# Routed experts: the order of the 128-slot and the 64-slot turns

## Chip, cores and metric

One core of one Trainium2 chip runs the kernel. The metric is the device time in microseconds. The kernel before took 2576.52, 2579.29 and 2581.18 us in three runs; the median is 2579.29 us.

## The reference, cut to what matters

The network is two blocks. The first has two layers of a hybrid mixer, a memory cross-attention and a feed-forward part; the second is an mLSTM/LRU block with product-key retrieval. The feed-forward part of the second layer is a mixture of 8 experts over 256 tokens of width 1024. Each token goes to its two best experts:

```
logits = (xt @ w_router).astype(jnp.float32)
top_vals, top_idx = lax.top_k(logits, TOP_K)          # TOP_K = 2 of N_EXPERTS = 8
...                                                   # softmax over the two gives the shares
y_e = (silu(x_e @ w_gate[e]) * (x_e @ w_up[e])) @ w_down[e]    # D_EXPERT = 3584
h = h + sum over the token's two experts of share * y_e
```

The last line and the one before it are the meaning of `moe_swiglu` in short form. The order in which the experts are computed does not enter into the result, apart from rounding of the sum.

## The kernel before, in words

**Turns.** The eight experts are computed in eight turns, 0 to 7. Each turn streams one expert's weights as 42 tiles of 1 MiB (`EXP_TILES`): 28 for gate and up (`GATE_UP`, four to a chunk of 512 hidden features, 7 chunks) and 14 for down (`DOWN`). Tile 0.0 is the first tile of turn 0.

**Two programs.** In a large turn (128 slots) the tokens are split in a high and a low part, each 128 columns wide, and every product of a weight tile is three matmuls: high by high (L862), high by low (L863), low by high (L864), 12 matmuls of 512 columns per tile. In a small turn (64 slots) the high and the low part of 64 tokens share one stationary operand of 128 columns (`xe_high` holds both, `he_pairs` the hidden ones), so that two matmuls are enough (L968, L969), 8 per tile; `folded_transposes` (L982) then adds the two halves. Both programs stream the same 42 tiles.

**A tile's way.** The SyncE queue issues the load of a tile (L1465) into one of 7 buffers (`RING`), as soon as TensorE has used the tile that was there seven tiles earlier. ScalarE rounds it to the high part (L1857), VectorE makes the low part (L2573), TensorE multiplies. ScalarE and VectorE are written out tile by tile with a lead of four tiles (`EXP_AHEAD`): at step j they first treat tile j+4 and then do the turn's other work of that step.

**Other work of a turn.** VectorE prepares the list of the next turn's tokens (`slot_lists`), GpSimd fetches their rows from `x_tokens` (L1570), TensorE transposes them, and VectorE copies them as high and low parts (`transposed_tokens`, L2593 and L2595), at step 33 of a large turn and step 31 of a small one. The width of these copies is set by the turn that comes next: 64 tokens or 128. At the end of a turn ScalarE scales the outputs (L1931 in a large turn, L1899 in a small one) and GpSimd adds them to `y_tokens` (L1578), in one scatter after a large turn and two after a small one.

**Order.** `ranks` (L2488 on) ranks the experts by their number of tokens. Expert 0 always has rank 0. `holds` marks which expert a turn holds; `order` gives SyncE the expert of each turn. The four experts of rank 0 to 3 get 128 slots and are turns 0 to 3; the other four get 64 slots and are turns 4 to 7. On each engine the large turns are one hardware loop (on VectorE a loop of three and one turn apart) and the small ones another (on VectorE and ScalarE with the last one apart). Tokens that find no slot would send the kernel into a second pass, which did not run here.

Of the kernel before, what the change touches and what calls it, by code (L numbers as in the profile page):

```python
# [13 lines left out]
P = 128  # L14
# [6 lines left out]
FF, N_EXP, EXP_W = 2816, 8, 3584  # L21
# [55 lines left out]
CHUNKS = EXP_W // 512  # L77
# [12 lines left out]
LIST_CHUNK = 3  # L90
CLEARS = 3
LARGE, HALF = 4, P // 2
EXP_MARKS = 2 * CHUNKS + DOWN - 1


# [131 lines left out]
def two_blocks(nc, t, out):  # L227
    with ExitStack() as ctx:
# [162 lines left out]
        room, order = small[:, 112:120], small[:, 120:128].bitcast(I32)  # L391
        turn_place_all = small[:, 202:202 + TB * (N_EXP + 1)].rearrange("p (b e) -> p b e", b=TB)
        turn_place, turn_share = turn_place_all[:, :, 0:N_EXP], pairs_of(32)
        rank_key, rank, excess, order_f = (std_row[:, 8 * i:8 * i + 8] for i in range(4))
        def by_rank(a):
            return a.rearrange("p (r e) -> p r e", r=N_EXP)
        holds, above, numbers = by_rank(std_row[:, 64:128]), by_rank(mean_row[:, 0:64]), by_rank(mean_row[:, 64:128])
# [164 lines left out]

        def rows_added(e, small=True):

            if small:
                return 16 * (CLEARS + LARGE + 2 * (e - LARGE))
            return 16 * (CLEARS + e)

        block = ctx.enter_context(nc.Block())

# [2 lines left out]
        def _(pe):  # L573
# [341 lines left out]
            def experts(n):  # L915
# [138 lines left out]
                pe.wait_ge(g.took_sems["v"], g.took["first", 4])  # L1054
                g.open_turns()
                if n == 0:
                    with pe.Fori(0, LARGE) as e:
                        turn(e, False)
                    pe.wait_ge(routing_ready, 1)
                    overflow = pe.value_load(extra_flag[0:1, 0:1], min_val=0, max_val=1)  # L1060
                    with pe.Fori(LARGE, N_EXP) as e:
                        turn(e, True)
                else:
                    with pe.Fori(0, N_EXP) as e:
                        turn(e, False)
# [463 lines left out]
        def _(pool):  # L1529
# [35 lines left out]
            pool.wait_ge(x_stored, 16)  # L1565
            g = passes[0]
            for e in range(N_EXP):
                kind, m = "s_" if e >= LARGE else "", HALF if e + 1 >= LARGE else P
                pool.wait_ge(g.took_sems["v"], g.took[kind + "lists"] + e * g.takes["v"])
                pool.indirect_dma_start(out=x_rows[0:m, :], out_offset=None, in_=x_tokens,  # L1570
                                        in_offset=bass.IndirectOffsetOnAxis(ap=token_at[0:m, :], axis=0)).then_inc(rows_gathered, 16)
                if e == N_EXP - 1:
                    break
                pool.wait_ge(g.took_sems["a"], g.took[kind + "down", 1] + e * g.takes["a"])
                for half in ((slice(0, HALF), slice(HALF, P)) if kind else (slice(0, P),)):
                    if half.start:
                        pool.wait_ge(y_done, rows_added(e) + 16)
                    pool.indirect_dma_start(out=y_tokens, out_offset=bass.IndirectOffsetOnAxis(ap=put_at[0:half.stop - (half.start or 0), :], axis=0), in_=ye[half, :],  # L1578
                                            in_offset=None, compute_op=ALU.add).then_inc(y_done, 16)
# [25 lines left out]
        def _(act):  # L1605
# [238 lines left out]
            def experts(n):  # L1844
# [90 lines left out]
                if n:  # L1935
# [4 lines left out]
                        expert(e, True)  # L1940
                    expert(N_EXP - 1, False)
                    return None
                with act.Fori(0, LARGE) as e:
                    expert(e, True)
                act.wait_ge(routing_ready, 1)
                overflow = act.value_load(extra_flag[0:1, 0:1], min_val=0, max_val=1)
                with act.Fori(LARGE, N_EXP - 1) as e:
                    small_expert(e, True)
                small_expert(N_EXP - 1, False)
                return overflow  # L1950

# [216 lines left out]
        def _(dve):  # L2168
# [310 lines left out]
            def eight(a, axis):  # L2479
                return a.unsqueeze(axis).to_broadcast([P, N_EXP, N_EXP])  # L2480
# [8 lines left out]
            def ranks():  # L2489

                iota8 = iota[:, 0:N_EXP]
                dve.wait_ge(dve_took, G.took["places"])
                step.now(dve.scalar_tensor_tensor(rank_key, counts, float(N_EXP), iota8, ALU.mult, ALU.subtract))
                step.now(dve.memset(rank_key[:, 0:1], 1.0e6))
                step.now(dve.tensor_tensor(above, eight(rank_key, 1), eight(rank_key, 2), ALU.is_gt))
                step.now(dve.tensor_reduce(rank, above, AX.X, ALU.add))
                step.then(dve.tensor_tensor(holds, eight(rank, 1), eight(iota8, 2), ALU.is_equal))
                step.now(dve.tensor_scalar(room, rank, float(LARGE) - 0.5, float(P - HALF), ALU.is_lt, ALU.mult))
                step.then(dve.tensor_scalar(room, room, float(HALF), None, ALU.add))
                step.now(dve.tensor_tensor(numbers, holds, eight(iota8, 1), ALU.mult))  # L2500
                step.then(dve.tensor_reduce(order_f, numbers, AX.X, ALU.add))
                step.now(dve.tensor_tensor(excess, counts, room, ALU.subtract))
                step.then(dve.tensor_copy(order, order_f))
                step.now(dve.tensor_reduce(most, excess, AX.X, ALU.max))
                dve.tensor_scalar(extra_flag[:, 0:1], most, 0.0, None, ALU.is_gt).then_inc(routing_ready, 1)
                dve.memset(turn_place_all[:, :, N_EXP:], -1.0)
                step.now(in_turns(turn_place, place))
# [14 lines left out]
            def experts(n):  # L2522
# [63 lines left out]
                def transposed_tokens(e, done, key, next_small):  # L2586

                    m = HALF if next_small else P
                    for i in range(KT // 2):
                        done((key, i))  # L2590
                        bank, s = pair(bank_in((key, i)), 2, P)[:, :, 0:m], slice(2 * i, 2 * i + 2)
                        high, low = xe_high[:, s, 0:m], xe_high[:, s, HALF:P] if next_small else xe_low[:, s, :]
                        dve.tensor_copy(high, bank).then_inc(g.x_high, 1)  # L2593
                        dve.wait_ge(g.x_high, 5 + e * (KT // 2) + i + 1)
                        took_it(dve.tensor_tensor(low, bank, high.bitcast(F32), ALU.subtract))  # L2595
# [9 lines left out]
                    dve.wait_ge(g.filled_ready, e + 1)  # L2605
                    took_it(dve.tensor_tensor(put_at, found[:, 2:3], rest_row, ALU.add))  # L2606

                def small_expert(e, follow):
                    def done(key):
                        dve.wait_ge(g.group_done, g.after[key] + e * g.in_turn)  # L2610

                    def multiply(c):
                        dve.wait_ge(g.activated, (e - LARGE) * CHUNKS + c + 1)
                        up = bank_in(("s_hidden", c))[:, 4 * HALF:8 * HALF].rearrange("p (a b) -> p a b", a=4)
                        took_it(dve.tensor_tensor(he_half[:, 4 * c:4 * c + 4, :], up, activated, ALU.mult))

                    def hidden(c):

                        dve.wait_ge(g.hidden_rounded, (e - LARGE) * CHUNKS + c + 1)
                        s = slice(4 * c, 4 * c + 4)  # L2620
                        dve.tensor_tensor(he_pairs[:, s, HALF:P], he_half[:, s, :], he_pairs[:, s, 0:HALF].bitcast(F32),
                                          ALU.subtract).then_inc(g.hidden_split, 1)

                    for j in range(EXP_TILES):
                        if j + EXP_AHEAD < EXP_TILES:
                            low_part(e, j + EXP_AHEAD)
                        elif follow:
                            low_part(e + 1, j + EXP_AHEAD - EXP_TILES)
                        c, step_ = divmod(j, 4)
                        if 0 < c < CHUNKS and step_ == 2:  # L2630
                            multiply(c - 1)
                        elif 1 < c <= CHUNKS and step_ == 0:
                            hidden(c - 2)
                        elif j == 1:
                            expert_columns(e, True)
                        elif j == 3:
                            expert_places(e)
                        elif j == 4 * LIST_CHUNK + 3:
                            slot_lists(e, done, "s_lists", True)
                        if j == GATE_UP:  # L2640
                            multiply(CHUNKS - 1)
                        elif j == GATE_UP + 2:
                            hidden(CHUNKS - 1)
                        elif j == GATE_UP + 3:
                            transposed_tokens(e, done, "s_gather", True)

                def expert(e, follow, next_small=False):
                    def done(key):
# [53 lines left out]
                dve.tensor_tensor(fold, ident[:, 0:HALF], ident[:, HALF:P], ALU.add)  # L2702
                dve.wait_ge(list_consts_ready, 1)
                dve.wait_ge(share_ready, 1)
                with dve.Fori(0, LARGE - 1) as e:
                    expert(e, True)
                dve.wait_ge(routing_ready, 1)
                overflow = dve.value_load(extra_flag[0:1, 0:1], min_val=0, max_val=1)
                expert(LARGE - 1, True, True)
                with dve.Fori(LARGE, N_EXP - 1) as e:  # L2710
                    small_expert(e, True)
                small_expert(N_EXP - 1, False)
                return overflow

            for l in range(DEPTH):
# [494 lines left out]
```

## Time and profile before

| | |
|---|---|
| median of three runs | 2579.29 us |
| span of the profiled execution | 2569.7 us |
| the three runs' own times | 2576.52, 2579.29, 2581.18 us; the page does not say which was profiled, so 6.8 to 11.5 us lie around its span |
| TensorE busy over the span | 2384.0 us (93%) |
| VectorE busy | 2009.7 us (78%) |
| ScalarE busy | 1256.6 us (49%) |
| moved by DMA | 786.10 MB, mean 306 GB/s |

The page's second part cuts the span in 40 slices of 64.2 us. The turns of the experts lie in slices 11 to 25, from about 656 to 1565 us. The span runs from the first to the last instruction; the device time also has what lies before and behind these. "Busy" of TensorE counts a matmul from its start to its modelled end, so a share of 100% says that it never stood idle, not that it computed at its peak.

### The profile page before, as it was taken

The page shows a single profiled execution, that of the slowest core. Times are in us where ns is not written, and L with a number is a line of the kernel's source. Part 1 is how long each engine was busy: PE and PEld are TensorE (multiplying, and loading weights), DVE is VectorE, ACT ScalarE, POOL GpSimd, SP SyncE. Part 2 cuts the span into 40 slices and gives each one's busy share as a digit, 9 for nine tenths or more (in the row PEclk, how much of TensorE's full clock was granted, in tenths as well). Part 3 has the DMA queues.
Part 4 walks back from the last instruction along what each step waited for, and adds up shares of the span by engine and source line. Part 5 has one row for each costly group of instructions (what it writes and reads, how often), then busy time and mean ns, then how long its engine had stood idle before and what let it go on. Part 6 is the DMA issues. An engine that isn't in the chain of part 4 may idle for free.

```text
span 2569.7 us, 32436 instructions
## 1 busy us (share of the span) xinstructions
PE 2384.0 (93%) x12064; PEld 1861.5 (72%) x12064; DVE 2009.7 (78%) x3035; ACT 1256.6 (49%) x1302; POOL 285.7 (11%) x305
## 2 busy tenths in 40 slices
PE   9999999999999999999899899999999987878786
PEld 8899999899788888877677678888985443323332
DVE  5766754865898888989999999666668887887875
ACT  2554332363777777878888886216421111111111
POOL 0000000000000000000000000000013433333341
PEclk9999999999999999999999999999999998899999
DMA  8454654541899999999999997531769999999997
GB/s 246 155 189 133 196 193 140 164 159 67 334 375 380 377 375 370 390 374 415 414 415 408 414 416 265 153 92 47 244 248 421 421 421 421 421 422 421 422 421 294
DMA packets 238447, 786.10 MB, mean 306 GB/s; under 512 B 24369, under 2 KB 154545, under 8 KB 162289
## 3 DMA queue, kind: packets, MB, share of 16 engines
q1 hardware_dynamic: 198000, 504.46, 53.1%
q0 software_dynamic: 39184, 276.58, 26.3%
q10 hardware_dynamic: 1136, 3.43, 0.3%
q8 instruction: 73, 1.20, 0.2%
q14 instruction: 54, 0.43, 0.0%
HBM read 777.08 MB, written 7.34 MB: 305 GB/s over the span
## 4 chain that ended last, share of the span: by engine, by line
PE 58%; DMA 22%; DVE 10%; issue 5%; ACT 4%; POOL 0%; DVEq 0%; ACTq 0%; SPq 0%
DMA dense_weights<-in_peer_rows,work 14%; DMA weight_tiles<-in_moe_tiles 7%; PE banks L862 7%; PE banks L864 7%; PE banks L863 7%; PE banks L728 5%; PE banks L1327 5%; PE banks L682 5%; PE banks L683 4%; PE banks L686 4%; PE banks L660 4%; DVE weight_tiles_low L2573 3%; ACT weight_tiles_high L1857 2%; PE banks L592 1%; PE banks L968 1%
## 5 line engine op out<-in xcount | busy, mean ns | idle before, releaser
L2573 DVE TENSOR_TENSOR weight_tiles_low<-weight_tiles,weight_tiles_high 128x2048 fp32r<-128x2048 f32 x335 | 761.5, 2288 | 72.7 <-ACT weight_tiles_high L1857 67.1
L1857 ACT ACTIVATE weight_tiles_high<-weight_tiles 128x2048 fp32r<-128x2048 f32 x332 | 635.5, 1918 | 149.4 <-DMA weight_tiles<-in_moe_tiles 144.7
L1327 PE MATMUL banks<-dense_weights,work 128*128 128x512 f32 x888 | 415.4, 618 | 57.9 <-DVE work L3104 57.5
L1327 PEld LDWEIGHTS banks<-dense_weights,work 128*128 128x128 f32 x888 | 173.0, 199 | 289.9 <-issue 201.1
L3094 DVE CUSTOM_DVE_ANT_0 dense_weights<-dense_weights,banks 128x1024 f32<-128x1024 f32 x222 | 266.5, 1217 | 68.2 <-DMA dense_weights<-in_peer_rows,work 67.3
L2205 DVE TENSOR_TENSOR weight_tiles_low<-weight_tiles,weight_tiles_high 128x2048 fp32r<-128x2048 f32 x93 | 212.2, 2289 | 129.2 <-ACT weight_tiles_high L1623 129.0
L2119 ACT ACTIVATE work<-work,small 128x2 f32<-128x2 f32 x129 | 38.1, 295 | 540.4 <-DVE work L3094 540.2
L1599 POOL DMA_INDIRECT dense_weights<-in_peer_rows,work x222 | 208.6, 940 | 588.0 <-DVE work L3050 315.0
L968 PE MATMUL banks<-weight_tiles_high,gathered_parts 128*128 128x512 f32 x448 | 183.8, 410 | 27.3 <-DVE weight_tiles_low L2573 26.8
L1623 ACT ACTIVATE weight_tiles_high<-weight_tiles 128x2048 fp32r<-128x2048 f32 x93 | 177.4, 1910 | 56.2 <-PE banks L864 29.5
L682 PE MATMUL banks<-weight_tiles_high 128*128 128x256 f32 x800 | 189.4, 281 | 5.1 <-issue 3.1
L683 PE MATMUL banks<-weight_tiles_high,weight_tiles_low 128*128 128x256 f32 x800 | 187.8, 280 | 0.0
L862 PE MATMUL banks<-weight_tiles_high,gathered_parts 128*128 128x512 f32 x448 | 176.4, 394 | 1.6 <-DVE gathered_parts L2584 1.1
L969 PE MATMUL banks<-weight_tiles_low,gathered_parts 128*128 128x512 f32 x448 | 175.6, 392 | 0.0
L864 PE MATMUL banks<-weight_tiles_high,gathered_parts 128*128 128x512 f32 x448 | 174.7, 390 | 0.0
L863 PE MATMUL banks<-weight_tiles_low,gathered_parts 128*128 128x512 f32 x448 | 174.4, 389 | 0.0
L682 PEld LDWEIGHTS banks<-weight_tiles_high 128*128 128x128 f32 x800 | 152.7, 191 | 5.7 <-issue 3.3
L683 PEld LDWEIGHTS banks<-weight_tiles_high,weight_tiles_low 128*128 128x128 f32 x800 | 152.6, 191 | 0.2
L968 PEld LDWEIGHTS banks<-weight_tiles_high,gathered_parts 128*128 128x128 f32 x448 | 84.0, 188 | 68.9 <-DVE weight_tiles_low L2573 52.8
L3104 DVE TENSOR_SCALAR work<-ident,work 128x128 f32<-128x128 f32 x256 | 79.2, 355 | 46.6 <-ACT work L2119 45.0
L1570 POOL DMA_INDIRECT work<-x_tokens,lists x8 | 18.0, 2248 | 848.0 <-DVE lists L2606 848.0
L728 PE MATMUL banks<-normed,weight_tiles 128*128 128x256 f32 (+1 forms) x512 | 111.7, 380 | 0.0
(508 smaller groups left out, 4467.9 us busy)
## 6 DMA issues: line engine op xcount, KB each, us to landing
weight_tiles<-in_moe_tiles SPq DMA_DIRECT2D x336, 1024.0 KB, 8.3
weight_tiles<-in_w_in SPq DMA_DIRECT2D x38, 1024.0 KB, 5.5
weight_tiles<-in_w_xkv SPq DMA_DIRECT2D x16, 1024.0 KB, 5.7
weight_tiles<-in_ffn_w_gate SPq DMA_DIRECT2D x11, 1024.0 KB, 5.3
weight_tiles<-in_ffn_w_up SPq DMA_DIRECT2D x11, 1024.0 KB, 5.3
weight_tiles<-in_ffn_w_down SPq DMA_DIRECT2D x11, 1024.0 KB, 5.0
weight_tiles<-in_w_xq SPq DMA_DIRECT2D x8, 1024.0 KB, 5.2
weight_tiles<-in_w_xo SPq DMA_DIRECT2D x8, 1024.0 KB, 5.2
```

What stands on the lines that cost most here:

```text
L682: pe.matmul(o, high[:, k, n_], high_x(k), start=(k == 0 and i == 0), stop=False)
L683: pe.matmul(o, low[:, k, n_], high_x(k), start=False, stop=False)
L728: mm = pe.matmul(bank[0:m, i * SEQ:(i + 1) * SEQ], w[:, k, i * P:i * P + m], x(k), start=(k == 0), stop=(k == KT - 1))
L862: pe.matmul(o, a_high, b_high, start=start, stop=False)
L863: pe.matmul(o, a_high, b_low, start=False, stop=False)
L864: return pe.matmul(o, a_low, b_high, start=False, stop=stop)
L968: pe.matmul(o, pairs, high, start=start, stop=False)
L1327: mm = pe.matmul(halves[half], diag[(first + j) % 8], pair_row(first + j)[:, 1, half * 512:(half + 1) * 512], start=False, stop=end and j ...
L1857: act.activation(high_tile(j), raw_tile(j), ACT.Copy).then_inc(g.high, 1)
L2205: dve.tensor_tensor(low_tiles[:, n % RING, 0:size], raw_tiles[:, n % RING, 0:size], high_tiles[:, j % HIGH_RING, 0:size].bitcast(F32), ALU ...
L2573: dve.tensor_tensor(low_tile(j), raw_tile(j), high_tile(j).bitcast(F32), ALU.subtract).then_inc(g.split, 1)
L3094: ins = dve.tensor_tensor_reduce(u_row, u_row, tokens(b), 1.0, 0.0, ALU.mult, ALU.add, dots[:, c:c + 1])
```

## The change

The turns alternate: even turns run the large program, odd turns the small one. Every engine's two loops become one loop over pairs of turns (`PAIRS` = 4), on VectorE and ScalarE over three pairs with the last pair apart. Ranks 0 to 3 keep 128 slots and become turns 0, 2, 4, 6; ranks 4 to 7 keep 64 and become turns 1, 3, 5, 7. `ranks` gets two small operations more that work out the turn of a rank. `rows_added` counts scatters in the new order. The number of turns of each kind, of tiles, matmuls, gathers and scatters is the same.

```diff
@@ rows_added
-            if small:
-                return 16 * (CLEARS + LARGE + 2 * (e - LARGE))
-            return 16 * (CLEARS + e)
+            return 16 * CLEARS + 24 * e - (8 if small else 0)
@@ TensorE
-                    with pe.Fori(0, LARGE) as e:
-                        turn(e, False)
+                    with pe.Fori(0, PAIRS) as p:
+                        turn(2 * p, False)
+                        turn(2 * p + 1, True)
                     pe.wait_ge(routing_ready, 1)
                     overflow = pe.value_load(extra_flag[0:1, 0:1], min_val=0, max_val=1)
-                    with pe.Fori(LARGE, N_EXP) as e:
-                        turn(e, True)
@@ GpSimd
-                kind, m = "s_" if e >= LARGE else "", HALF if e + 1 >= LARGE else P
+                kind, m = ("s_", HALF if e == N_EXP - 1 else P) if e % 2 else ("", HALF)
@@ ScalarE
-                with act.Fori(0, LARGE) as e:
-                    expert(e, True)
+                with act.Fori(0, PAIRS - 1) as p:
+                    expert(2 * p, True)
+                    small_expert(2 * p + 1, True)
                 act.wait_ge(routing_ready, 1)
                 overflow = act.value_load(extra_flag[0:1, 0:1], min_val=0, max_val=1)
-                with act.Fori(LARGE, N_EXP - 1) as e:
-                    small_expert(e, True)
+                expert(N_EXP - 2, True)
                 small_expert(N_EXP - 1, False)
@@ VectorE, ranks
-                step.then(dve.tensor_tensor(holds, eight(rank, 1), eight(iota8, 2), ALU.is_equal))
                 step.now(dve.tensor_scalar(room, rank, float(LARGE) - 0.5, float(P - HALF), ALU.is_lt, ALU.mult))
                 step.then(dve.tensor_scalar(room, room, float(HALF), None, ALU.add))
+                step.now(dve.tensor_scalar(late, rank, float(LARGE) - 0.5, float(N_EXP - 1), ALU.is_gt, ALU.mult))
+                step.now(dve.scalar_tensor_tensor(turn_at, rank, 2.0, late, ALU.mult, ALU.subtract))
+                step.now(dve.tensor_tensor(holds, eight(turn_at, 1), eight(iota8, 2), ALU.is_equal))
@@ VectorE, small_expert
-                            transposed_tokens(e, done, "s_gather", True)
+                            transposed_tokens(e, done, "s_gather", not follow)
@@ VectorE, experts
-                with dve.Fori(0, LARGE - 1) as e:
-                    expert(e, True)
+                with dve.Fori(0, PAIRS - 1) as p:
+                    expert(2 * p, True, True)
+                    small_expert(2 * p + 1, p, True)
                 dve.wait_ge(routing_ready, 1)
                 overflow = dve.value_load(extra_flag[0:1, 0:1], min_val=0, max_val=1)
-                expert(LARGE - 1, True, True)
-                with dve.Fori(LARGE, N_EXP - 1) as e:
-                    small_expert(e, True)
-                small_expert(N_EXP - 1, False)
+                expert(N_EXP - 2, True, True)
+                small_expert(N_EXP - 1, PAIRS - 1, False)
```

On TensorE, this is the end of the loop of large turns (turn 3's last matmul and what follows it) in the kernel before. L1060 reads the flag for the second pass; the matmuls behind it are turn 4's first ones.

```order
L863 MATMUL banks<-weight_tiles_low,work_parts 128x512
L864 MATMUL banks<-weight_tiles_high,work_parts 128x512
L937 REGISTER_ALU
L1057 REGISTER_ALU
L1057 COMPARE_AND_BRANCH
L1060 TENSOR_LOAD extra_flag
L1060 ISA x2
L1061 UNCONDITIONAL_BRANCH
L1061 ISA
L957 ISA
L968 MATMUL banks<-weight_tiles_high,gathered_parts 128x512
L969 MATMUL banks<-weight_tiles_low,gathered_parts 128x512
```

And in the changed kernel, at the same place of the program (the end of a large turn; its line numbers are lower by one):

```order
L862 MATMUL banks<-weight_tiles_low,work_parts 128x512
L863 MATMUL banks<-weight_tiles_high,work_parts 128x512
L936 REGISTER_ALU
L115 ISA
L956 ISA
L967 MATMUL banks<-weight_tiles_high,gathered_parts 128x512
L968 MATMUL banks<-weight_tiles_low,gathered_parts 128x512
```

The small turn's matmuls now follow each large turn inside the loop, and the branch back stands behind each small turn. The reading of the flag has moved behind the last turn.

On VectorE, this is step 31 of a small turn in its loop in the kernel before: the copies of the next turn's tokens between the low parts of two weight tiles (`gathered_parts` holds the tokens, `2x64` is two features' groups of 64 tokens).

```order
L2573 TENSOR_TENSOR weight_tiles_low<-weight_tiles,weight_tiles_high 128x2048
L2610 REGISTER_ALU
L2593 CAST gathered_parts<-banks 128x2x64
L2594 ISA
L2595 TENSOR_TENSOR gathered_parts<-banks,gathered_parts 128x2x64
L2610 REGISTER_ALU
L2593 CAST gathered_parts<-banks 128x2x64
L2594 REGISTER_ALU
L2595 TENSOR_TENSOR gathered_parts<-banks,gathered_parts 128x2x64
```

The same place in the changed kernel:

```order
L2573 TENSOR_TENSOR weight_tiles_low<-weight_tiles,weight_tiles_high 128x2048
L2610 REGISTER_ALU
L2593 CAST gathered_parts<-banks 128x256
L2594 ISA
L2595 TENSOR_TENSOR gathered_parts<-banks,gathered_parts 128x256
L2610 REGISTER_ALU
L2593 CAST gathered_parts<-banks 128x256
L2594 REGISTER_ALU
L2595 TENSOR_TENSOR gathered_parts<-banks,gathered_parts 128x256
```

The copies of a small turn in the loop are now 256 wide, since a large turn follows it; those of every large turn are 2x64 wide, which before was so for turn 3 alone.

## Rows read from the trace of the kernel before

**Rows 1.** The page, part 2: the span in 40 slices.
```profile
GB/s 246 155 189 133 196 193 140 164 159 67 334 375 380 377 375 370 390 374 415 414 415 408 414 416 265 153 92 47 244 248 421 421 421 421 421 422 421 422 421 294
```
**Rows 2.** Busy time of the engines in turns 1 to 7, one row per turn.
```profile
core 0: us, PE busy (x) PEld busy (x) DVE busy (x) ACT busy (x) POOL busy (x), PEclk, DMA share, GB/s
775.50:894.90 119.40, 119.40 (x550) 99.08 (x549) 107.24 (x74) 93.96 (x68) 3.01 (x2) 1.00 0.96 377
894.90:1014.30 119.40, 119.40 (x550) 99.08 (x549) 105.65 (x73) 92.49 (x67) 2.57 (x2) 1.00 0.98 375
1014.30:1133.70 119.40, 119.40 (x550) 99.08 (x549) 107.00 (x75) 94.51 (x69) 5.08 (x2) 1.00 0.98 377
1133.70:1239.40 105.70, 97.35 (x466) 77.15 (x464) 97.04 (x73) 88.06 (x70) 4.52 (x2) 0.98 1.01 411
1239.40:1347.30 107.90, 97.79 (x464) 75.28 (x464) 101.86 (x74) 91.92 (x72) 6.41 (x3) 1.00 1.01 414
1347.30:1455.60 108.30, 98.05 (x465) 75.43 (x464) 102.15 (x75) 91.91 (x72) 6.36 (x3) 1.00 1.01 413
1455.60:1564.80 109.20, 98.36 (x465) 76.92 (x465) 100.28 (x75) 88.13 (x71) 6.32 (x3) 0.98 0.95 386
```
**Rows 3.** TensorE's first gate matmul: turns 4, 5, 7 (first and last start, us).
```profile
L968 PE MATMUL banks<-weight_tiles_high,gathered_parts x114: 387/391/504, 1133.7 to 1239.9; 128*128 128x512 f32 x114
...
L968 PE MATMUL banks<-weight_tiles_high,gathered_parts x113: 387/393/504, 1239.3 to 1347.6; 128*128 128x512 f32 x113
...
L968 PE MATMUL banks<-weight_tiles_high,gathered_parts x112: 387/393/504, 1455.9 to 1528.3; 128*128 128x512 f32 x112
```
**Rows 4.** Tile loads (L1465), issue to landing: 1010 to 1133 us, then 1289 to 1397.
```profile
DMA to landing us min/median/max: 4.7/5.4/8.8
...
DMA to landing us min/median/max: 8.7/10.7/13.2
```
**Rows 5.** Timeline of TensorE from turn 3 into turn 4.
```profile
1133.44 0.39 PE L864 MATMUL banks<-weight_tiles_high,work_parts 128*128 128x512 f32 x1
1133.67 0.39 PE L968 MATMUL banks<-weight_tiles_high,gathered_parts 128*128 128x512 f32 x1
...
1148.86 0.50 PE L968 MATMUL banks<-weight_tiles_high,gathered_parts 128*128 128x512 f32 x1 [1.85 <-DVE weight_tiles_low L2573]
```
**Rows 6.** Stretches: turn 4's start and rest; two drops of the clock.
```profile
1133.70:1147.00 13.30, 13.12 (x57) 10.22 (x55) 9.16 (x9) 9.38 (x8) 1.76 (x1) 1.00 1.02 371
1147.00:1239.30 92.30, 84.16 (x409) 66.85 (x408) 87.79 (x65) 78.68 (x62) 2.76 (x1) 0.98 1.01 417
...
1226.80:1230.10 3.30, 3.30 (x10) 2.53 (x9) 3.30 (x2) 2.40 (x2) 0.00 (x0) 0.50 1.03 425
1551.10:1554.40 3.30, 3.17 (x8) 2.50 (x9) 3.30 (x3) 2.08 (x2) 0.00 (x0) 0.50 1.02 423
```
**Rows 7.** Timeline of VectorE: turn 0's token copies, then turn 5's.
```profile
753.82 0.42 DVE L2593 CAST gathered_parts<-banks 128x256 fp32r<-128x256 f32 x1
...
756.98 8.89 DVE L2573 TENSOR_TENSOR weight_tiles_low<-weight_tiles,weight_tiles_high 128x2048 fp32r<-128x2048 f32 x4
...
1329.93 0.28 DVE L2593 CAST gathered_parts<-banks 128x128 fp32r<-128x128 f32 x1
...
1332.03 20.02 DVE L2573 TENSOR_TENSOR weight_tiles_low<-weight_tiles,weight_tiles_high 128x2048 fp32r<-128x2048 f32 x9
```
**Rows 8.** Waits in turn 0 (656 to 775 us).
```profile
PE banks L862 <- DVE weight_tiles_low L2573: 0.5, 1, 0.5
```
**Rows 9.** Turn 0's start: `ranks` on VectorE, and TensorE's wait.
```profile
659.83 0.22 DVE L2497 TENSOR_TENSOR std<-std,iota 128x64 f32<-128x64 f32 x1
659.97 0.16 DVE L2498 TENSOR_SCALAR small<-std 128x8 f32<-128x8 f32 x1
...
664.41 8.90 DVE L2573 TENSOR_TENSOR weight_tiles_low<-weight_tiles,weight_tiles_high 128x2048 fp32r<-128x2048 f32 x4 [0.18 <-issue]
...
666.76 0.50 PE L862 MATMUL banks<-weight_tiles_high,gathered_parts 128*128 128x512 f32 x1 [0.55 <-DVE weight_tiles_low L2573]
```

More of the change, by code:

```diff
@@ L92 @@
 LARGE, HALF = 4, P // 2
+PAIRS = N_EXP // 2
 EXP_MARKS = 2 * CHUNKS + DOWN - 1
@@ L393, in two_blocks @@
         turn_place, turn_share = turn_place_all[:, :, 0:N_EXP], pairs_of(32)
-        rank_key, rank, excess, order_f = (std_row[:, 8 * i:8 * i + 8] for i in range(4))
+        rank_key, rank, excess, order_f, late, turn_at = (std_row[:, 8 * i:8 * i + 8] for i in range(6))
         def by_rank(a):
@@ L2606, in slot_lists, with small_expert @@
                     took_it(dve.tensor_tensor(put_at, found[:, 2:3], rest_row, ALU.add))
-                def small_expert(e, follow):
+                def small_expert(e, p, follow):
                     def done(key):
@@ L2612, in multiply @@
                     def multiply(c):
-                        dve.wait_ge(g.activated, (e - LARGE) * CHUNKS + c + 1)
+                        dve.wait_ge(g.activated, p * CHUNKS + c + 1)
                         up = bank_in(("s_hidden", c))[:, 4 * HALF:8 * HALF].rearrange("p (a b) -> p a b", a=4)
@@ L2617, in hidden @@
                     def hidden(c):
-                        dve.wait_ge(g.hidden_rounded, (e - LARGE) * CHUNKS + c + 1)
+                        dve.wait_ge(g.hidden_rounded, p * CHUNKS + c + 1)
                         s = slice(4 * c, 4 * c + 4)
```

## The prediction, made before the changed kernel ran

> **What bounds the kernel now.** I first read the page's slices for where the experts lie: in slices 12 to 18 the DMA rate stands near 377 GB/s and in slices 19 to 24 near 414 [rows 1]. Then I cut this stretch at the turns. A large turn takes 119.4 us and TensorE is busy for all of it; a small turn takes 105.7 to 109.2 us and TensorE is idle for 8.4 to 10.8 us of it [rows 2]. So the two programs have different limits. The large one is bound by TensorE: the DMAs bring 377 GB/s, and 411 to 414 GB/s in the small turns shows that they could bring more. The small one is bound by its supply: 42 tiles of 1.049 MB at 417 GB/s, the rate of the steady part of turn 4 [rows 6], are 105.6 us, and the scatters and gathers take the DMAs too. VectorE is close behind, busy for 102 of 108 us.
>
> Between the two lies the ring of 7 buffers. A buffer is loaded again when TensorE has used its tile, so a tile's round is 7 tiles long: 7 x 119.4 / 42 = 19.9 us in a large turn, 7 x 108.3 / 42 = 18.0 in a small one. Of this the load takes 5.4 us in a large turn and 10.7 in a small one, where loads queue [rows 4]. What is left, 14.5 against 7.3 us, is the time from landing to use, and the large turn's extra of 7.2 us is lead: tiles that are ready and wait for TensorE. A small turn behind a large one spends this lead. The trace has one such place, and it is the model for the change. TensorE goes from turn 3's last matmul to turn 4's first with no gap (1133.44, 1133.67: 0.23 us, the step of the stream), and its first wait of more than 0.2 us ends at 1148.86 [rows 5].
>
> **What the change is worth, part by part.**
>
> Small turn behind large. By first matmuls turn 4 takes 1239.3 - 1133.7 = 105.6 us, turn 5 takes 1347.6 - 1239.3 = 108.3, and turn 6 takes 1455.9 - 1347.6 = 108.3 [rows 3]. The lead is thus worth 2.7 us by the end of the turn. Its first seven tiles took 13.3 us in place of 18.0, which is 4.7 us saved, but in this stretch the DMAs moved only 371 GB/s, and 2.0 us are given back as the buffers run short [rows 6]. Before, turns 5, 6 and 7 stood behind a small turn. After, all four small turns stand behind a large one: 3 x 2.7 = 8.1 us saved.
>
> Large turn behind small. This is new in the trace three times (turns 2, 4, 6) and has two parts. One is the width of the token copies at the end of the small turn. Eight copies at 128x256 take 756.98 - 753.82 = 3.16 us, eight at 128x128 take 1332.03 - 1329.93 = 2.10 us [rows 7]. Behind these copies VectorE runs nine low parts back to back (20.02 us, 2.2 us each), which reach three tiles into the next turn [rows 7]; TensorE waits for each of them, so nothing hides the 1.06 us: the next turn's first tile is that much later. It costs 3 x 1.06 = 3.2 us. The large turns 0, 2 and 4 get narrower copies in exchange; there VectorE has the lead before it, and I count nothing for it (at most the same 3.2 us, at least nothing).
>
> The other part is the start of the large turn without a lead. A large tile takes TensorE 2.84 us (119.4 / 42). VectorE needs 107.2 / 42 = 2.55 us per tile with everything it does in a large turn, and the DMAs 1.049 / 417 = 2.5 us. Both are faster than TensorE, so from the first tile on it should find the next one ready and the lead should build by 0.3 us a tile, full before the turn ends (7.2 / 0.3 = 24 tiles of 42). Turn 0 shows such a start on VectorE's side: at 666.76 TensorE takes tile 0.4 right as its low part comes [rows 9], and up to the turn's end it waits for VectorE no more (one wait, 0.5 us) [rows 8]. What turn 0 does not show is a full DMA queue at the same time. I take nothing for this part. The lower bound is nothing, as there is no stall to remove in a large turn. The upper bound is that the whole lead has to be bought by waiting, 7.2 us a turn.
>
> ScalarE has at such a start 1.4 us of output scaling and perhaps the reload of an activation table; it has 25 us to spare in a large turn [rows 2] and is tiles ahead. I cost it at nothing, and if its cover went it would be inside the upper bound just named.
>
> `ranks`. Two small operations are added and one loses its overlap. Dependent ones of this size start some 0.14 us apart without a wait (659.83, 659.97) [rows 9] and somewhat more with one; three such steps are about 0.5 us. They stand before the low parts of tiles 0.4 to 0.7 (664.41), and TensorE waits 0.55 us there for tile 0.4 [rows 9]. So all of it goes on the path: 0.5 us, between 0.3 and 0.8. A TensorE-bound turn follows and cannot win it back.
>
> Moved at no cost: the flag's reading on TensorE now stands behind turn 7. TensorE's sequencer ran ahead of the matmuls at its old place, where no gap shows [rows 5]; at the new one I take nothing, at most 1 us. The number of scatters and gathers is the same, and so are their bytes; three of the large turns now start beside two scatters in place of one, with the same bytes.
>
> Sum: -8.1 + 3.2 + 0.5 = -4.4 us. The profiled execution's span of 2569.7 us would become 2565.3. What lies around the span is not touched, so the median of 2579.3 becomes 2574.9 us, 0.17% less.
>
> **The clock.** At VectorE's copies TensorE waits longest, and in turns 4 and 7 the granted clock then fell to 0.50, the 1.2 GHz level, for some 3.3 us; in turns 5 and 6 it did not [rows 2, 6]. It fell 13 us before the turn's end, where TensorE has time to spare, and turn 4 was still the shortest. The Trainium skill (TensorE: Matmul & The Clock Gate, "What's actually happening") has it that the clock is granted by recent activity. By that rule the wait that grows by 1.06 us makes drops likelier in three turns; where they fell before they cost nothing. A drop that reached into a large turn would cost half its length, 1.7 us.
>
> **The rivals.**
>
> *The lead is kept* (faster). If the 4.7 us of turn 4's first seven tiles are not given back, the three turns save 14.1 us and the sum is -14.1 + 3.7 = -10.4: 2568.9 us. For it: a small turn that starts early puts its loads into the queue early. Against it: turn 4 gave back 2.0 us, and the changed turns repeat it.
>
> *The large turn starves* (slower). TensorE, without a lead, waits at each place where VectorE does something else: the columns and picks at steps 4 and 6, the hidden parts, and the loads that two scatters hold up. It decides if tiles come slower than 2.84 us in the first ten tiles of turns 2, 4 and 6. With half of the bound, 3.6 us a turn, it is 10.8 us on the sum: +6.4, 2585.7 us; with all of it +17. For it: VectorE's margin is only 0.3 us a tile. Against it: the first turn [rows 8].
>
> *All is given back* (no change). The buffers' lead is one and the same time, and what the small turn spends the next large one has to load again, beside its own tiles. If the costs at the border are 1.5 us more per pair than my count, the whole is zero: 2579.3 us. The Trainium skill (DMA: Bandwidth & Descriptors, "Where 436 GB/s comes from") names a limit of some 358 GB/s on the HBM side for loads into SBUF. By that rule both programs would be bound by the same DMA rate and their order would be worth nothing, 2579.3 us. The trace disagrees: 414 GB/s in small turns, 377 in large ones with TensorE never idle [rows 2].
>
> That the change does not do what it says can be left out: turns, tiles and matmuls are the same, and no wait is tied to a turn's kind.
>
> **Chances and range.** Forecast 0.58, with its own range 2572 to 2578; no change 0.17; lead kept 0.12; starving 0.13. About 0.2%, 5.2 us, is what a measurement of this kernel can tell from no change; the three runs before spread over 4.7 us. The forecast's own range reaches over that bound on the faster side: 0.58 x 0.45 = 0.26, with the lead kept 0.12 it makes 0.38 for faster. Slower has the starving rival's greater part, 0.12. The rest, 0.50, is the same. For 8 in 10 I take 2566 to 2583 us: down to the lead kept with some us below it, up to a starving turn at a third of its bound.
>
> **What the profile after will show.** Right: turns 1, 3 and 5 of 106.7 us by first matmuls and turns 2, 4 and 6 of 119.4 with TensorE busy in all of it; the copies of turns 1, 3, 5 at 128x256 and 3.2 us long; the DMA rate in turn pairs near 377 and 411. Wrong: waits of TensorE for VectorE in the first ten tiles of turns 2, 4 and 6 (starving); small turns below 105 us (lead kept); small turns of 108 us (no lead at all); or a difference outside 656 to 1565 us.

## The result, and the profile after

The changed kernel took 2594.81 us (median of 4 runs, 2591.70 to 2598.07) beside 2578.55 us for the kernel before. The ratio is 1.0070 with a 95% interval of 1.0053 to 1.0086: it is slower by 16 us, where 4.4 us less had been forecast. The profiled execution has a span of 2591.2 us and a time of 2593.05 us, so only 1.9 us lie around a span, not the 6.8 to 11.5 us of the table before. The profiled execution before, with its span of 2569.7 us, was a quick one of its kind, and the two spans are further apart (21.5 us) than the medians. Of the 21.5 us, 13.4 lie in the turns of the experts, which take 923.2 us (660.4 to 1583.6) instead of 909.8 (655.0 to 1564.8). Of the rest, 5.4 us lie ahead of turn 0, before any loop over turns; in the ten kernels profiled here turn 0 begins anywhere from 653.1 to 660.4 us, in the old order as in the new one. So the turns are compared by themselves.

The turns by TensorE's first gate matmul, one row per turn from turn 1 on, answer to [rows 2]:

```profile
core 0: us, PE busy (x) PEld busy (x) DVE busy (x) ACT busy (x) POOL busy (x), PEclk, DMA share, GB/s
781.30:892.50 111.20, 96.79 (x466) 75.59 (x465) 103.00 (x75) 92.82 (x74) 4.96 (x2) 0.99 1.01 412
892.50:1014.10 121.60, 121.60 (x549) 100.69 (x550) 104.82 (x73) 91.26 (x65) 6.56 (x3) 0.98 0.96 361
1014.10:1125.20 111.10, 97.80 (x465) 76.95 (x463) 103.96 (x75) 92.84 (x73) 5.16 (x2) 0.98 1.01 412
1125.20:1246.40 121.20, 121.16 (x548) 100.37 (x549) 106.99 (x75) 93.79 (x69) 8.28 (x3) 0.99 0.96 370
1246.40:1357.30 110.90, 97.70 (x465) 78.27 (x463) 102.17 (x74) 91.93 (x73) 4.40 (x2) 0.97 1.01 409
1357.30:1478.50 121.20, 121.16 (x548) 100.33 (x549) 107.11 (x75) 91.15 (x66) 6.89 (x3) 0.99 0.96 369
1478.50:1583.60 105.10, 97.44 (x464) 76.90 (x463) 94.59 (x72) 84.27 (x68) 4.31 (x2) 0.98 0.95 385
```

Turns 1, 3 and 5 take 111 us instead of the 106.7 forecast, turns 2, 4 and 6 take 121.2 to 121.6 instead of 119.4, and the last small turn, which no turn follows, takes 105. Within the turns all of the loss is at the three places where a small turn ends and a large one begins. TensorE's timeline at the first of them:

```profile
887.19 0.39 PE L967 MATMUL banks<-weight_tiles_high,work_parts 128*128 128x512 f32 x1
887.42 0.39 PE L968 MATMUL banks<-weight_tiles_low,work_parts 128*128 128x512 f32 x1
892.49 0.79 PE L861 MATMUL banks<-weight_tiles_high,gathered_parts 128*128 128x512 f32 x1 [4.68 <-ACT work L1897]
893.08 0.63 PE L862 MATMUL banks<-weight_tiles_low,gathered_parts 128*128 128x512 f32 x1
```

TensorE stands still for 4.68 us, and its next matmuls take 0.63 us each instead of 0.39. The releaser named, ScalarE's output scaling, is only the last semaphore event before; the next tile is no reason either. VectorE's and ScalarE's timelines over the same time:

```profile
883.36 11.09 DVE L2573 TENSOR_TENSOR weight_tiles_low<-weight_tiles,weight_tiles_high 128x2048 fp32r<-128x2048 f32 x5
898.26 2.29 DVE L2573 TENSOR_TENSOR weight_tiles_low<-weight_tiles,weight_tiles_high 128x2048 fp32r<-128x2048 f32 x1 [3.81 <-ACT weight_tiles_high L1855]
```
```profile
889.31 1.91 ACT L1855 ACTIVATE weight_tiles_high<-weight_tiles 128x2048 fp32r<-128x2048 f32 x1 [0.57 <-DMA weight_tiles<-in_moe_tiles]
891.13 1.25 ACT L1897 ACTIVATE work<-banks,lists 128x512 f32<-128x512 f32 x2
895.02 1.28 ACT L1855 ACT_TABLE_LOAD   x1 [2.64 <-issue]
896.31 3.72 ACT L1855 ACTIVATE weight_tiles_high<-weight_tiles 128x2048 fp32r<-128x2048 f32 x2
```

The five low parts of VectorE's first row are those of tiles 1.41 and 2.0 to 2.3, the last of them done at 894.5. Tile 2.0 had been ready since about 887.8, and TensorE began it at 892.49. At the same place ScalarE stands for 2.64 us with "issue" named, that is, with nothing to wait for. At the two later places TensorE's row names no releaser but issue as well (4.28 and 4.31 us).

What both engines have there is the branch back to the start of the loop, and the trace has its duration. (A q behind an engine's name marks what its sequencer does, the part that issues the engine's instructions.) On TensorE, the loop's line in the changed kernel, and in the kernel before (loop of the large turns):

```profile
L1056 PEldq COMPARE_BRANCH  x4: 83/5904/6256, 885.9 to 1582.1; - x4
...
L1057 PEldq COMPARE_BRANCH  x4: 76/210/244, 771.6 to 1129.8; - x4
```

The last of the four branches is not taken (83 and 76 ns). The three taken ones last 5.9 to 6.3 us instead of 0.21 to 0.24. The first starts at 885.90, while matmuls issued ahead still run until 887.8, and the next matmul comes behind it at 892.49. On ScalarE the branch itself is short (54 ns), but the first instruction of the loop's next pass (FUSED_REGOPS) comes 5.1 us behind it; in the kernel before (loop of the small turns) it came after 0.27 us:

```profile
L1941 ACTq COMPARE_BRANCH  x1: 54/54/54, 889.7 to 889.7; - x1
L1941 ACTq FUSED_REGOPS  x1: 68/68/68, 894.8 to 894.8; - x1
...
L1947 ACTq COMPARE_BRANCH  x1: 54/54/54, 1242.5 to 1242.5; - x1
L1947 ACTq FUSED_REGOPS  x1: 59/59/59, 1242.7 to 1242.7; - x1
```

The clock behind the stop, a stretch whose granted clock is 0.50, the 1.2 GHz level:

```profile
890.00:896.80 6.80, 4.31 (x10) 3.46 (x11) 4.45 (x3) 4.15 (x5) 3.13 (x1) 0.50 0.94 339
```

The page's DMA queues show what the loop does. Queue 8 brings blocks of 16 KB of instructions; before it brought 73 of them, now 103:

```profile
q8 instruction: 73, 1.20, 0.2%
```
```profile
q8 instruction: 103, 1.69, 0.3%
```

In the trace before, no such block comes from 755 to 1145 us (large turns 1 to 3) nor from 1230 to 1565 us: the loop's code stayed loaded. Now they come through all turns, mostly every 20 to 30 us, and at each branch back one starts while TensorE stands still (889.6 us at the first). Blocks of 8 KB on a second instruction queue, number 14, do the same in ScalarE's two stops (893.2 and 1127.5 us); in the kernel with TensorE's and ScalarE's loops written out (below) none comes from 883.1 to 945.5 us. Counting TensorE's instructions in the trace, matmuls, weight loads, register operations and waits, gives about 1180 for a large turn, 1017 for a small one and 2190 for the new body; a few records may be missing.

### The profile page after: what moved, and what is told of

It is laid out like the page before. It is cut to its first block, busy times and chain, and to the rows that moved or that the text cites. A ratio compares the mean times of both kernels' runs of the same rounds, so it can differ in the third digit from the quotient of the medians.

```text
span 2591.2 us, 32356 instructions
## 1 busy us (share of the span) xinstructions
PE 2398.1 (93%) x12064; PEld 1877.9 (72%) x12064; DVE 2011.6 (78%) x3037; ACT 1253.6 (48%) x1300; POOL 292.5 (11%) x305
## 4 chain that ended last, share of the span: by engine, by line
PE 59%; DMA 19%; DVE 12%; issue 5%; ACT 4%; POOL 0%; DVEq 0%; ACTq 0%; SPq 0%
DMA dense_weights<-in_peer_rows,work 12%; PE banks L861 7%; PE banks L863 7%; PE banks L862 7%; DMA weight_tiles<-in_moe_tiles 6%; PE banks L727 5%; PE banks L1325 5%; PE banks L681 5%; PE banks L682 5%; PE banks L685 5%; PE banks L659 4%; DVE weight_tiles_low L2573 4%; ACT weight_tiles_high L1855 2%; PE banks L591 1%; DVE dense_weights L3093 1%
```

## Experiments

Two theories were put against each other. Theory 1: the body of the loop is too long to stay loaded and every branch back has to fetch its first code. Theory 2, a rival of the prediction: the large turn starves without a lead in its buffers. Times are medians; every ratio is to the kernel before on the same chip, with its 95% interval. The kernel before took 2578.60 us beside the first four kernels and 2575.53 us beside the last four, so their times are compared by ratio and not as they stand.

**TensorE unrolled.**

```diff
-                    with pe.Fori(0, PAIRS) as p:
+                    for p in range(PAIRS):
                         turn(2 * p, False)
                         turn(2 * p + 1, True)
```

> The changed kernel, with TensorE's loop over the four pairs of turns written out; every other engine as in the changed kernel. Theory 1 (code fetch at the backward branch): the pair's body is some 2190 instructions on TensorE, more than stays loaded, so each of three branches back stops TensorE for 4.3 to 4.7 us and the clock falls behind it; without the branch turns 2, 4 and 6 go from 126.0 to 119.4 us, the kernel from 2594.8 to about 2574 us, 0.2% under the kernel before. Theory 2 (the large turn starves without a lead in its buffers): turns 2, 4 and 6 stay at 125 to 126 us and the kernel at 2592 to 2597 us.

Measured: 2578.40 us, ratio 0.9998 (0.9987 to 1.0008). The branch taken away on one engine gives back all that the change had cost, though the kernel stays 4 us above the 2574 of the expectation. (The 126.0 us there count the stop with the large turn; by first matmuls it lies in the small turn before.) Its turns 1, 2, 3, 4 and 6:

```profile
777.10:884.10 107.00, 96.32 (x465) 75.66 (x464) 98.43 (x73) 88.75 (x71) 4.90 (x2) 1.00 1.01 412
884.10:1005.80 121.70, 119.86 (x548) 99.12 (x549) 108.02 (x75) 94.09 (x68) 5.58 (x3) 1.00 0.97 376
1005.80:1113.10 107.30, 97.08 (x465) 75.55 (x463) 100.57 (x74) 91.14 (x72) 5.17 (x2) 1.00 1.01 413
1113.10:1234.50 121.40, 119.86 (x548) 99.14 (x549) 110.81 (x76) 96.33 (x70) 7.36 (x3) 1.00 0.97 379
...
1341.90:1461.40 119.50, 119.50 (x549) 99.26 (x550) 110.82 (x76) 94.01 (x68) 15.43 (x3) 1.00 0.99 385
```

The small turns are at 107 us. Turns 2 and 4 still take 2 us too long, now at a full clock and with TensorE idle for 1.5 to 1.8 us, and turn 6 does not. Turn 6 is the one that ScalarE and VectorE reach without a branch back. ScalarE's timeline in front of turn 2, and in front of turn 6:

```profile
887.51 1.25 ACT L1897 ACTIVATE work<-banks,lists 128x512 f32<-128x512 f32 x2
891.41 1.28 ACT L1855 ACT_TABLE_LOAD   x1 [2.66 <-issue]
892.71 3.71 ACT L1855 ACTIVATE weight_tiles_high<-weight_tiles 128x2048 fp32r<-128x2048 f32 x2
...
1345.01 1.25 ACT L1897 ACTIVATE work<-banks,lists 128x512 f32<-128x512 f32 x2
1346.14 3.92 ACT L1855 ACTIVATE weight_tiles_high<-weight_tiles 128x2048 fp32r<-128x2048 f32 x2
```

2.66 us of stop and a load of the activation table (ACT_TABLE_LOAD) of 1.28 us make tile 2.4 late. The table load stood in the loop of large turns before too (776.34 us), where the engine did not stop ahead of it; in front of turn 6 there is neither. TensorE waits for the tile:

```profile
897.10 0.47 PE L861 MATMUL banks<-weight_tiles_high,gathered_parts 128*128 128x512 f32 x1 [1.80 <-DVE weight_tiles_low L2573]
```

**The branch moved behind the large turn.**

```diff
-                    with pe.Fori(0, PAIRS) as p:
-                        turn(2 * p, False)
-                        turn(2 * p + 1, True)
+                    turn(0, False)
+                    with pe.Fori(0, PAIRS - 1) as p:
+                        turn(2 * p + 1, True)
+                        turn(2 * p + 2, False)
+                    turn(N_EXP - 1, True)
```

> Alternating order as in the changed kernel, TensorE's loop shifted by one turn: turn 0 apart, a loop of three over (small, large), turn 7 apart. Same body size, same number of backward branches less one, but they stand between a large and a small turn. Theory 1: TensorE still stops for some 4.5 us two times, but now where a lead of 7 us and 8 us of idle time in the small turn take it up; turns 2, 4, 6 take 119.4 us, turns 3 and 5 at most 2 us more than 106.7, kernel 2574 to 2580 us. Theory 2: as the changed kernel, 2592 to 2597 us, since every large turn still follows a small one.

Measured: 2581.99 us, ratio 1.0014 (1.0005 to 1.0024), 2 us above the range of theory 1 and 10 under that of theory 2. TensorE's stop at the branch, the one before turn 3:

```profile
1008.51 0.79 PE L967 MATMUL banks<-weight_tiles_high,gathered_parts 128*128 128x512 f32 x1 [2.75 <-ACT work L1931]
```

The branch takes 6.5 us as before, from 1001.74, but TensorE has matmuls until 1005.76 to work off: 4.0 us where it had 1.9 behind a small turn. So 2.75 us are left (1.79 at the second branch), and the small turns behind them take 105.1 us, 1.7 less than the 106.8 without any branch. But the expectation missed the large turns: with the stop behind them turns 2 and 4 take 127.5 and 128.5 us instead of 119.4. In each TensorE also waits behind ScalarE's branch, which still stands in front of these turns and which I had left out, for 3.0 and 3.9 us, with the lower clock behind the wait. All turns together take 919.6 us, 3.6 less than in the changed kernel, and there are two branches back where it has three. So the place of the branch helps, but how much of the better ratio is due to it alone this kernel does not show.

**The old order with long bodies.**

```diff
-                    with pe.Fori(0, LARGE) as e:
-                        turn(e, False)
+                    with pe.Fori(0, LARGE // 2) as p:
+                        turn(2 * p, False)
+                        turn(2 * p + 1, False)
...
-                    with pe.Fori(LARGE, N_EXP) as e:
-                        turn(e, True)
+                    with pe.Fori(LARGE // 2, N_EXP // 2) as p:
+                        turn(2 * p, True)
+                        turn(2 * p + 1, True)
```

> The kernel before (four large turns, then four small), with TensorE's two loops over two turns per body: (large, large) twice, (small, small) twice. Order unchanged. Theory 1: the body of two large turns is some 2360 instructions and is fetched again at its one branch back (turn 1 to 2): TensorE stops some 4.5 us there and the clock falls, turn 2 becomes 125 to 126 us and the kernel is 6 us slower than before. The body of two small ones is some 2030 and may stay loaded: no stop between turns 5 and 6, or one that the small turn's idle time takes up. Theory 2: no large turn follows a small one, so nothing changes: 2578 us.

Measured: 2582.38 us, ratio 1.0021 (1.0009 to 1.0034). This is the stop without any change of order. Turns 1 and 2, 5 and 6, and TensorE behind the two branches:

```profile
775.70:897.30 121.60, 119.57 (x550) 98.90 (x548) 108.06 (x74) 95.31 (x70) 3.59 (x3) 1.00 0.98 378
897.30:1018.50 121.20, 121.20 (x549) 100.36 (x550) 104.19 (x73) 90.28 (x65) 4.56 (x2) 0.99 0.96 365
...
1243.70:1356.50 112.80, 98.30 (x465) 75.30 (x465) 106.72 (x76) 94.26 (x74) 6.41 (x3) 0.99 1.01 413
1356.50:1462.90 106.40, 100.02 (x465) 78.91 (x465) 97.55 (x74) 89.69 (x71) 6.39 (x3) 0.96 1.01 407
```
```profile
897.29 0.63 PE L862 MATMUL banks<-weight_tiles_high,gathered_parts 128*128 128x512 f32 x1 [2.03 <-ACT work L1933]
...
1356.49 0.79 PE L968 MATMUL banks<-weight_tiles_high,gathered_parts 128*128 128x512 f32 x1 [4.47 <-issue]
```

The two branches take 5.8 and 6.1 us. Between two large turns TensorE's queue hides 4.0 us of it (2.03 us idle; the two turns together are 4.0 us longer, not the 6 expected), between two small ones 1.9 (4.47 us idle), and the supply then gives some back, 219.2 us for the two turns instead of 216.6. My expectation that the body of two small turns, some 2030 instructions, stays loaded was wrong.

**The old order, all unrolled.** `for e in range(...)` in place of every loop over turns on TensorE, ScalarE and VectorE.

> The kernel before with all loops over turns written out on TensorE, ScalarE and VectorE. It is the control for unrolling as such. Both theories: within 2 us of the kernel before (2576 to 2581 us), since its short loops showed no stop at their branches; code of all turns is now fetched once through.

Measured: 2577.14 us, ratio 0.9999 (0.9989 to 1.0009). Unrolling as such neither costs nor gives, to within 0.1%.

**The new order, all unrolled.**

```diff
-                    with pe.Fori(0, PAIRS) as p:
+                    for p in range(PAIRS):
...
-                with act.Fori(0, PAIRS - 1) as p:
+                for p in range(PAIRS - 1):
...
-                with dve.Fori(0, PAIRS - 1) as p:
+                for p in range(PAIRS - 1):
```

> Alternating order with no loop over turns at all: TensorE, ScalarE and VectorE written out. In the run with TensorE alone unrolled, turns 2 and 4 still took 121.7 and 121.4 us and turn 6, which ScalarE and VectorE reach without a branch, 119.5. Theory 1 (code fetch, on ScalarE too): turns 2 and 4 fall to 119.5 us, the kernel is 4 us faster than with TensorE alone unrolled and 3 to 4.5 us under the kernel before (the size the prediction gave to the order): about 2574.5 us, ratio 0.9985. Theory 2 (the order itself costs what it gives, and unrolling ScalarE changes nothing): 2578.5 us, turns 2 and 4 at 121.5.

Measured: 2570.12 us beside 2575.53 us, ratio 0.9976 (0.9964 to 0.9988). With the next one it is the fastest version that computes everything, and it beats both kernels. The 0.9985 of theory 1 lies inside the interval. In its profiled execution the large turns 2, 4 and 6 take 119.4 to 119.6 us as forecast, but the small turns 1, 3 and 5 take 108.6, 106.9 and 108.2.

**The same with VectorE's loop kept.**

> Alternating order, TensorE and ScalarE written out, VectorE still in its loop of three pairs. If the 2.1 us that turns 2 and 4 still lost come from ScalarE's branch back (2.66 us with nothing to wait for, then a table load of 1.28 us, before it rounds tile 4), this kernel equals the one with all unrolled: turns 2 and 4 at 119.5 us, about 2574.5. If VectorE's branch is the one, they stay at 121.5 and the kernel at 2578.5 us.

Measured: 2569.89 us, ratio 0.9978 (0.9967 to 0.9988), equal to the one before. VectorE's branch, over about 287 instructions, costs nothing, and behind it there is no stop: the next pass begins 0.39 us later.

```profile
L2705 DVEq COMPARE_BRANCH  x1: 72/72/72, 887.9 to 887.9; - x1
L2705 DVEq FUSED_REGOPS  x1: 74/74/74, 888.3 to 888.3; - x1
```

All turns of this kernel from 1 on:

```profile
777.60:884.30 106.70, 97.33 (x465) 77.01 (x465) 98.50 (x73) 89.01 (x71) 4.86 (x2) 0.98 1.01 412
884.30:1003.80 119.50, 119.48 (x548) 99.17 (x549) 109.58 (x75) 93.21 (x67) 6.59 (x3) 1.00 0.98 385
1003.80:1110.70 106.90, 97.39 (x466) 77.08 (x465) 99.48 (x74) 89.86 (x72) 5.36 (x2) 0.98 1.01 411
1110.70:1230.20 119.50, 119.50 (x548) 99.14 (x549) 110.68 (x76) 94.11 (x68) 8.40 (x3) 1.00 0.98 387
1230.20:1337.00 106.80, 96.87 (x465) 76.85 (x464) 98.13 (x73) 88.41 (x71) 4.59 (x2) 0.98 1.01 407
1337.00:1456.60 119.60, 119.59 (x549) 99.22 (x550) 110.71 (x76) 94.79 (x68) 6.60 (x3) 1.00 1.00 390
1456.60:1561.40 104.80, 97.90 (x464) 80.32 (x463) 94.25 (x72) 83.89 (x68) 4.40 (x2) 0.95 0.96 386
```

Small turns of 106.7 to 106.9 us and large ones of 119.5 to 119.6 with TensorE busy throughout are the numbers of the forecast, to 0.2 us. All eight turns take 905.1 us, where 909.8 - 4.4 = 905.4 had been forecast. That is one execution; the kernel with everything unrolled took 908.9 us in its own. At the border in front of turn 2 TensorE waits for 0.18 us:

```profile
884.32 0.47 PE L861 MATMUL banks<-weight_tiles_high,gathered_parts 128*128 128x512 f32 x1 [0.18 <-DVE weight_tiles_low L2573]
```

**TensorE's loop kept, ScalarE and VectorE unrolled.**

> The other way round: TensorE in its loop of four pairs, ScalarE and VectorE written out. If TensorE's stop (4.3 to 4.7 us and a lower clock behind it) is the larger part and ScalarE's is hidden behind it, the kernel is 0 to 2 us faster than the changed one: 2592 to 2595 us, ratio to before 1.0055 to 1.0065. If the two add up, it is 4 us or more faster: under 2591 us.

Measured: 2589.63 us, ratio 1.0054 (1.0039 to 1.0069). TensorE's stop is there in full (4.83 us in front of turn 2). The interval overlaps that of the changed kernel, and the ratio lies at the border of the two expectations (1.0055), so the times can't tell a gain of 4 us from none. The trace shows no gain: turns 1 and 2 take 112.1 and 121.2 us here and 111.2 and 121.6 in the changed kernel. That agrees with ScalarE's stop being hidden behind TensorE's as long as both are there.

**Narrow copies.** The new order, all unrolled, and each small turn leaves the upper 64 slots of the large turn behind it out of the computation:

```diff
-                            transposed_tokens(e, done, "s_gather", not follow)
+                            transposed_tokens(e, done, "s_gather", True)
```

> All unrolled, and the small turns copy only 64 of the next turn's 128 tokens, as if a small turn followed: the upper 64 slots of turns 2, 4 and 6 are left out of the computation (their copies keep older values). It prices the wide copies alone, 1.06 us in turns 1, 3 and 5. If these are on the path as the prediction had it, turns 1, 3 and 5 take 1.0 us less each than with all unrolled, the kernel 3.2 us less (ratio to before 0.9973). If VectorE's lag is covered by something else, nothing changes.

Measured: 2566.86 us, ratio 0.9965 (0.9954 to 0.9977), 3.3 us under the same kernel with wide copies, though the two intervals overlap. Turns 1, 3 and 5 took 106.0, 105.3 and 107.5 us, beside 108.6, 106.9 and 108.2 with wide copies, 4.9 us less in all; beside the 106.7, 106.9 and 106.8 of the kernel with VectorE's loop kept, whose copies are as wide, it is 1.6 us. The 3 x 1.06 us of the sum lie between the two. These single executions differ among themselves by as much, so the size is not shown more closely.

## Why the prediction was wrong

**The step that failed** is the start of the large turn behind a small one, for which the prediction said "I take nothing for this part". It looked only at the supply of tiles. At that place the hardware loop's branch had come to stand, as the rows of TensorE's order under the change tell, and I did not price it. The branch lasts 5.9 to 6.3 us where it lasted 0.2. It costs 4.3 to 4.7 us of stop on TensorE and about 2 us more through the lower clock, three times. In the profiled executions that is 111.1 - 106.8 = 4.3 us per small turn and 121.3 - 119.5 = 1.8 us per large turn, 3 x 6.1 = 18.3 us between the changed kernel and the one with TensorE and ScalarE unrolled. Measured by medians the distance is about 24 us, ratio 1.0070 against 0.9978; the intervals leave room from 0.65% to 1.2%, that is from 17 to 31 us, and the turns' own 18.3 lies inside. The upper bound of 7.2 us a turn does reach over the 6.1 us, but by luck: it was made for waits on tiles, and in the changed kernel TensorE waited for none in turns 2, 4 and 6.

The Trainium skill has this rule, and the prediction did not draw on it: "Runtime: NRT & Kernel Launch", section "Instruction fetch mechanics", says that a taken branch whose target is not in the two pages loaded (of 256 instructions each) has to fetch that page before it goes on, and gives the instruction memory as 2048 instructions for TensorE and 512 for the others. By the 2048 the trace agrees for the new body of about 2190 on TensorE and for bodies of about 1180 and 1017, which showed no stop; by the two pages it disagrees, since these would have stopped too. It disagrees in two more places: two small turns, some 2030 instructions, stopped for 4.47 us, and ScalarE's body of 336 to 338 stopped for 2.6 to 3.4 us.

**The rival that came out nearest in time was right for the wrong reason.** The starving turn gave +6 to +17 us at the same three places. But large turns behind small ones do not starve: with the branches gone on TensorE and ScalarE they take 119.5 us, TensorE busy for all of it.

**Point by point.** Small behind large, 2.7 us saved: right in the kernel with TensorE and ScalarE unrolled, 106.8 us with the wide copies where 105.6 + 1.06 had been worked out; with everything unrolled two of the three turns took 108.6 and 108.2 in the profiled execution. The lead rebuilt within the large turn: right, since turns 3 and 5 are as short as turn 1. The wide copies, 1.06 us each on the path: right in length, since in the changed kernel eight of them run from 869.19 to 872.36, 3.17 us; that all of it lies on the path agrees with the narrow copies but is not shown to the tenth. ScalarE at no cost: wrong; its stop costs 2 us in turns 2 and 4 as soon as TensorE's is gone, and is covered before. `ranks`: turn 0 took 120.9 us after and 120.4 before, the 0.5 us of the sum, though single executions of the other versions in the new order show 120.8 to 121.3. The clock: it falls behind the stop and reaches into the large turn, which the prediction had priced at 1.7 us and thought of only as a risk of the copies. The order's whole effect: -6.2 us by ratio (0.9976, -9.3 to -3.1 us) where -4.4 had been worked out; against the old order unrolled (0.9999) it is much the same. The profiled turns give -4.7 us with VectorE's loop kept and -0.9 with everything unrolled. So the runs show that the new order gains, by 3 to 9 us with 4.4 inside, but not more closely than that.

## What to carry to other kernels

A loop over two bodies is longer than either, and whether its code stays loaded is a property to check in the profile like any other: look how long the branch at the loop's line lasts and how soon the next pass begins behind it, whether the instruction queues bring blocks in the middle of the loop, and count the instructions of the body. If they do, write the loop out on that engine, or try the branch where the engine has issued ahead or where the next work has slack. When a change moves a loop's border, price the border on each engine by itself, since the loss of one can hide the loss of another.

## What the runs showed of the hardware that was not expected

A branch back whose target is no longer loaded takes 5.5 to 6.5 us on TensorE, where one of a short loop takes 0.2. TensorE then stands still for 4.3 to 5.0 us behind a small turn, where 1.9 us of matmuls had been issued ahead, and for 1.8 to 2.75 us behind a large one, where 4.0 us had been. On ScalarE the next pass begins 5.1 to 5.9 us behind the branch instead of 0.3, and the engine stands still for 2.6 to 3.4 us. Straight code is fetched without a stop: unrolled, queue 8 brings 97 blocks instead of 73 and the time does not change.

```profile
q8 instruction: 97, 1.59, 0.3%
```

Why ScalarE's body of 336 to 338 instructions and the pair of small turns on TensorE were not kept was not settled; how blocks lie against the body's start may have a part in it, which no run here tells.
